# First projection chunk by halves, and the conv front end prepared in the last chunk of the projection

## What is computed

```python
x = layer_norm(x, ln0_g, ln0_b)
h = x @ w_in                                   # 1024 -> 384 value | 384 gate | 384 pool | 256 query
a = h_val * sigmoid(h_gate)
a = causal_depthwise_conv(a, conv_w, conv_b)   # 31 taps
a = silu(layer_norm(a, conv_ln_g, conv_ln_b))
p = pool_mixer(h_pool, pool_w, pool_scale)     # trailing means over 2, 4, 8, 16 frames
mo = memory_cross_attention(q, mem, w_mk, w_mv)  # 4 heads, 256 memory tokens
y = concatenate([a, p, mo]) @ w_out
x = layer_norm(alpha * x + y, ln1_g, ln1_b)
y = conv_ffn(x, w_up, ffn_conv_w, ffn_conv_b, w_down)
x = layer_norm(alpha * x + y, ln2_g, ln2_b)
```

## Time and profile before

| | |
|---|---|
| median of 3 runs | 2025.26 us (2025.09 to 2026.36) |
| profiled execution | 2024.7 us, its span 2023.0 us |
| mean granted TensorE clock | 0.978 |
| TensorE matmul busy | 1887.1 us, 93% of the span |
| VectorE / ScalarE / GpSimd busy | 1484.2 / 941.1 / 264.1 us |
| costliest line | L2072, three groups of 1848 matmuls, 723 to 726 us busy each |

### The profile page before, as it was taken

The page is one execution under the profiler, slowest core; times in us unless marked ns, Lnnn a source line. Parts: engine busy times, 40 slices in busy tenths (PEclk is TensorE's granted clock), DMA queues, the critical chain, the costliest instruction groups (busy, mean ns, idle before and its releaser), DMA issues.

```text
span 2023.0 us, 26054 instructions
## 1 busy us (share of the span) xinstructions
PE 1887.1 (93%) x8626; PEld 1563.7 (77%) x8626; DVE 1484.2 (73%) x1892; ACT 941.1 (47%) x1598; POOL 264.1 (13%) x339
## 2 busy tenths in 40 slices
PE   4999988869999899999999899999999897999997
PEld 4778868748878778888888688888887686887786
DVE  6444018658888798888887888787787767657899
ACT  3111114545555466556556655555556335234331
POOL 1111014101212322222221011000000000000111
PEclk9999999979999999999999899999999998999999
DMA  6432125444353743433434333122124567547543
GB/s 218 156 110 68 47 71 188 151 141 147 114 181 112 275 161 128 142 139 130 145 135 172 140 132 128 73 93 83 73 93 162 182 212 271 187 151 273 185 160 125
DMA packets 171786, 296.12 MB, mean 146 GB/s; under 512 B 11712, under 2 KB 106176, under 8 KB 171712
## 3 DMA queue, kind: packets, MB, share of 16 engines
q1 hardware_dynamic: 171712, 295.18, 41.9%
HBM read 189.23 MB, written 105.91 MB: 146 GB/s over the span
## 4 chain that ended last, share of the span: by engine, by line
PE 64%; DVE 12%; DMA 3%; issue 3%; ACT 3%; POOL 0%; SPq 0%; DVEq 0%; ACTq 0%; POOLq 0%
PE banks L2072 55%; PE banks L967 4%; DVE mov_lo L2269 1%; PE banks L985 1%; DMA mov_raw<-wdown_sums_scratch 1%; DVE sta_lo L2265 1%; PE banks L949 1%; PE banks L900 1%; DMA y_scratch<-up_and_out 1%; DMA mov_raw<-x_operands 1%; PE banks L931 1%; DVE up_and_out L2303 1%; DVE probs L1436 1%; PE banks L1030 0%; DVE up_and_out L2300 0%
## 5 line engine op out<-in xcount | busy, mean ns | idle before, releaser
L2072 PE MATMUL banks<-mov_hi,sta_hi 128*128 128x512 f32 x1848 | 726.3, 393 | 37.9 <-ACT banks L2148 19.6
L2072 PE MATMUL banks<-mov_lo,sta_hi 128*128 128x512 f32 x1848 | 723.5, 392 | 0.0
L2072 PE MATMUL banks<-mov_hi,sta_lo 128*128 128x512 f32 x1848 | 723.4, 391 | 0.0
L2072 PEld LDWEIGHTS banks<-mov_hi,sta_hi 128*128 128x128 f32 x1848 | 350.0, 189 | 117.3 <-ACT banks L2148 21.3
L2072 PEld LDWEIGHTS banks<-mov_hi,sta_lo 128*128 128x128 f32 x1848 | 349.6, 189 | 73.5
L2072 PEld LDWEIGHTS banks<-mov_lo,sta_hi 128*128 128x128 f32 x1848 | 350.2, 189 | 72.4
L2265 DVE TENSOR_TENSOR sta_lo<-sta_raw,sta_hi 128x512 fp32r<-128x512 f32 (+1 forms) x340 | 224.1, 675 | 61.2 <-ACT sta_hi L2134 59.3
L2134 ACT ACTIVATE sta_hi<-sta_raw 128x512 fp32r<-128x512 f32 (+1 forms) x340 | 198.8, 611 | 133.9 <-PE banks L2072 102.2
L261 PE MATMUL wb<-x0t_hi,win_hi 128*128 128x512 f32 x352 | 140.5, 399 | 2.9 <-DVE x0t_lo L353 2.9
L261 PE MATMUL wb<-x0t_hi,win_lo 128*128 128x512 f32 x352 | 138.3, 393 | 0.0
L261 PE MATMUL wb<-x0t_lo,win_hi 128*128 128x512 f32 x352 | 138.1, 392 | 0.0
(11 more groups left out here) (219 smaller groups left out, 2692.6 us busy)
## 6 DMA issues: line engine op xcount, KB each, us to landing
sta_raw<-in_w_up SPq DMA_DIRECT2D x88, 512.0 KB, 4.1
hidden_scratch<-up_and_out SPq DMA_DIRECT2D x44, 512.0 KB, 2.6
y_scratch<-up_and_out SPq DMA_DIRECT2D x16, 1024.0 KB, 7.5
sta_raw<-hidden_scratch SPq DMA_DIRECT2D x32, 512.0 KB, 4.5
up_and_out<-y_scratch SPq DMA_DIRECT2D x16, 1024.0 KB, 4.9
x_operands<-x_operands_out SPq DMA_DIRECT2D x56, 256.0 KB, 4.2
mov_raw<-x_operands SPq DMA_DIRECT2D x14, 1024.0 KB, 6.9
mov_raw<-in_w_down SPq DMA_DIRECT2D x44, 256.0 KB, 4.7
```

Of the source, the lines that this page charges most:

```text
L2072: last = pe.matmul(psum, w, x, start=(start and k == 0 and i == 0), stop=(stop and k == m - 1 and i == 2), skip_group_check=True)
```

## The change

In block 1:

- SyncE issues weight pieces 0 to 3 ahead of x tiles 2 and 3.
- TensorE does `turn` 0 to 3, then `project_half(0)` and `project_half(1)` in place of the first four tiles of chunk 0: half of the frames (256 columns) at a time, and within it weight piece by weight piece (two input slices, four output tiles: 24 matmuls each), with `turn` 4 to 7 behind pieces 1 and 2 of the first half. ScalarE's and VectorE's orders follow. `turn` of chunk 1 comes in twos behind tiles 7 to 10, and VectorE does all four layer norms of chunk 1 before its eight low parts.
- In the last chunk SyncE loads taps, conv bias and pairs 0 to 3, GpSimd makes the block mask, ScalarE and VectorE split taps and pairs 0 to 2, and VectorE makes bands 0 to 9. The buffers of the two blocks are placed by hand so that these go where the projection has finished.
- SyncE's wait for the query stores goes from the end of block 1 into block 2, behind nothing and ahead of the loads of pair 4 and the memory tokens.

In block 2:

- What is done already falls away at its start. The ten band buffers are reused for bands 10 to 15, then three of them for the rest; bands 10 to 23 are made in steps 1, 2, 3 and 6 to 10. The first `w_out` slice to be loaded is another one.

```diff
-        def first_turn(c):
-            return 1 if c else JT - 2 * TT
+        def turns_behind(c, n):
+            if c + 1 == NCH:
+                return ()
+            if c == 0:
+                return (2 * (n - JT + TT), 2 * (n - JT + TT) + 1) if n >= JT - TT else ()
+            return (n - 1,) if 1 <= n <= 2 * TT else ()
...
-            load_w(0)
+            for i in range(4):
+                load_w(i)
             load_x(2)
-            load_w(1)
             load_x(3)
-            for i in range(2, 7):
+            for i in range(4, 7):
                 load_w(i)
...
+                if c + 1 == NCH:
+                    for i, s in enumerate(x0_stored):
+                        sp.wait_ge(s, 16 * len(range(i, SEQ // P, RING)))
+                    sp.wait_ge(tp_ready, 2 * SEQ // P)
+                    opening.load_taps(sp)
                 for t in range(CT):
...
                     store_gated(c, t)
+                    if c + 1 == NCH and t == 0:
+                        sp.wait_ge(glu_stored[0], 16 * NCH)
+                        for m in range(4):
+                            opening.load_pair(sp, m)
...
-            sp.wait_ge(q_stored, 16 * QT * NCH)
...
+            def project_half(half):
+                tok = slice(half * CH // 2, (half + 1) * CH // 2)
+                pe.wait_ge(lo_done, TT * (half + 1))
+                for piece in range(4):
+                    pe.wait_ge(win_lo, piece + 1)
+                    for n in range(4):
+                        cols = slice(n * P, (n + 1) * P)
+                        for k in (2 * piece, 2 * piece + 1):
+                            pairs = exact_parts(w_hi[0][:, k, cols], w_lo[0][:, k, cols], xt_hi[0][:, k, tok], xt_lo[0][:, k, tok])
+                            for i, (w, x) in enumerate(pairs):
+                                last = pe.matmul(wb[:, n, tok], w, x, start=(k == 0 and i == 0), stop=(k == KT - 1 and i == 2), skip_group_check=True)
+                        if half and piece == 3:
+                            last.then_inc(proj, 1)
+                    if half == 0 and piece in (1, 2):
+                        turn(0, 2 * piece + 2)
+                        turn(0, 2 * piece + 3)
+
             pe.wait_ge(ident_ok, 2)
-            for i in range(2 * TT):
+            for i in range(TT):
                 turn(0, i)
+            project_half(0)
+            project_half(1)
             for c in range(NCH):
                 for n in range(JT):
-                    project(c, n)
+                    if c or n >= 4:
+                        project(c, n)
...
@@ ScalarE, block 1 @@
-            for u in range(TT):
-                weights_hi(u)
-                split_hi(0, 2 * u)
-                split_hi(0, 2 * u + 1)
-            for i in range(4, 7):
+            weights_hi(0)
+            weights_hi(1)
+            split_hi(0, 0)
+            split_hi(0, 1)
+            weights_hi(2)
+            split_hi(0, 2)
+            split_hi(0, 3)
+            for i in range(3, 7):
                 weights_hi(i)
+            for i in range(TT, 2 * TT):
+                split_hi(0, i)
...
@@ VectorE, block 1 @@
             layer_norm_end(0)
-            layer_norm(2)
             layer_norm_end(1)
             weights_lo(0)
             lows(0, 0, 1)
+            weights_lo(1)
+            lows(0, 2, 3)
+            layer_norm(2)
             layer_norm(3)
             layer_norm_end(2)
-            weights_lo(1)
-            lows(0, 2, 3)
+            weights_lo(2)
+            weights_lo(3)
             layer_norm_end(3)
-            weights_lo(2)
             lows(0, 4, 5)
-            weights_lo(3)
+            weights_lo(4)
             lows(0, 6, 7)
-            for i in range(4, 7):
+            for i in range(5, 7):
                 weights_lo(i)
...
+                if c + 1 == NCH:
+                    opening.taps_lo(dve, 0)
+                    opening.taps_lo(dve, 1)
+                    dve.wait_ge(opening.mask_made, 3)
+                    dve.wait_ge(proj, JT * c)
+                    for n in range(4):
+                        opening.conv_band(dve, n)
                     gate(c, 0)
+                    gate(c, 1)
+                    dve.wait_ge(proj, JT * c + 4)
+                    for n in range(4, 7):
+                        opening.conv_band(dve, n)
+                    opening.clear_leads(dve)
+                    gate(c, 2)
+                    for m in range(3):
+                        opening.pair_lo(dve, m)
+                    dve.wait_ge(proj, JT * c + 8)
+                    for n in range(7, 10):
+                        opening.conv_band(dve, n)
+                    continue
...
@@ VectorE, block 2 @@
+            bands_at = {1: (10, 11), 2: (12, 13), 3: (14, 15), 6: (16, 17), 7: (18,), 8: (19,), 9: (20, 21), 10: (22, 23)}
             for m in range(NP):
-                if is_conv(m):
-                    conv_band(2 * ORDER[m] + 3)
-                    conv_band(2 * ORDER[m] + 4)
+                for n in bands_at.get(m, ()):
+                    conv_band(dve, n)
```

More of the change, by code:

```diff
@@ L234, in _ @@
                 pool.tensor_tensor(s[:, 14:15], s[:, 13:14], half[:, 0:1], ALU.pow).then_inc(ln_rstd, 1)
+            pool.wait_ge(x0_stored[0], 16 * len(range(0, SEQ // P, RING)))
+            pool.wait_ge(tp_ready, 2 * SEQ // P)
+            opening.block_mask(pool)
         @block.tensor
@@ L323, in _ @@
                             weights_hi(i)
[L324 to L326 removed]
+                    for i in turns_behind(c, n):
+                        split_hi(c + 1, i)
+                    if c + 1 == NCH and n == 0:
+                        opening.taps_hi(act, 0)
+                        opening.taps_hi(act, 1)
+                    if c + 1 == NCH and n == 5:
+                        for m in range(3):
+                            opening.pair_hi(act, m)
         @block.vector
@@ L546, in mixing_phase @@
         last_xt = sem("last_x1T_stored")
-        ffn = ffn_phase(a, xop_d, x1_d, h_d, wdt_d, part_d, out, at, sem, banks)
-        block = ctx.enter_context(nc.Block())
         wo_more = late[:, 0:2 * D].rearrange("p (a d) -> p a d", a=2)
@@ L609, in groups_done, with band_place, band_before @@
             return 2 * ORDER.index(n // 2) + n % 2 + 1
+        def band_place(n):
+            return n if n < 10 else n - 10 if n < 13 else (3, 4, 5)[n - 13] if n < 16 else (n - 16) % 3
+        def band_before(n):
+            return max((g for g in range(n) if band_place(g) == band_place(n)), default=None)
         def bank_of(m):
@@ new lines, in block_mask @@
+        def block_mask(pool):
+            pool.memset(same, 1.0).then_inc(bands, 1)
+            pool.wait_ge(bands, 1)
+            same_cr = same.rearrange("p (c r) -> p c r", r=PHASES)
+            pool.affine_select(out=same_cr, in_=same_cr, compare_op=ALU.is_ge, fill=0.0, base=0,
+                               pattern=[[-PHASES, GROUP], [0, PHASES]], channel_multiplier=1).then_inc(bands, 1)
+            pool.wait_ge(bands, 2)
+            pool.affine_select(out=same_cr, in_=same_cr, compare_op=ALU.is_ge, fill=0.0, base=PHASES - 1,
+                               pattern=[[PHASES, GROUP], [0, PHASES]], channel_multiplier=-1).then_inc(bands, 1)
@@ new lines, in conv_band @@
+        def conv_band(dve, n):
+            dve.wait_ge(gt_lo, 1 + (n >= TAPS_FIRST))
+            if band_before(n) is not None:
+                dve.wait_ge(g_mm, groups_done(band_before(n)))
+            out = gt[band_place(n)][:, :].rearrange("p (e c r) -> p e c r", c=GROUP, r=PHASES)
+            tap = tap_parts[:, n, :, :].rearrange("p e (s o r) -> p (e s) o r", o=1, r=PHASES).to_broadcast((P, 2 * LAGS, GROUP, PHASES))
+            mask = same.rearrange("p (o c r) -> p o c r", o=1, r=PHASES).to_broadcast((P, 2 * LAGS, GROUP, PHASES))
+            dve.tensor_tensor(out, tap, mask, ALU.mult).then_inc(gt_ok, 1)
@@ L645, in _ @@
+        opening = Opening(load_taps, load_pair, block_mask, bands, taps_hi, pair_hi, taps_lo, clear_leads, pair_lo, conv_band)
+        q_stored = project_phase(nc, a, x0_d, cp_d, mix_d, used, at, banks, opening)
+        ffn = ffn_phase(a, xop_d, x1_d, h_d, wdt_d, part_d, out, at, sem, banks)
+        block = ctx.enter_context(nc.Block())
         @block.sync
```

208 lines of the change are left out of this document (90 added, 118 removed).

## The result

| | before | after |
|---|---|---|
| median of 4 runs on one chip | 2025.57 us (2025.09 to 2026.36) | 2012.50 us (2009.71 to 2015.45) |
| ratio, 95% interval | | 0.9935 [0.9920, 0.9950] |
| profiled execution, its span | 2024.7, 2023.0 us | 2015.45, 2013.7 us |
| mean granted TensorE clock | 0.978 | 0.976 |

The change makes the kernel 13.1 us faster; forecast were 13.7 us and 2011.5. The profiled execution is the slowest of the four of after. Its chain of waits is still TensorE's (`PE 64%`), so the up-projection sets most of the time as before.

What follows compares the result with a forecast made beforehand. TensorE bounds the kernel, mostly in an untouched up-projection, so gains come from its idle or slow stretches before about 345 us. Opening 6.3 plus boundary 7.4 is 13.7 us, giving 2011.5; likeliest range 2009 to 2014, 8 in 10 2006 to 2018.

Steps and rivals of the forecast that it cites:

- 6.3 + 7.4 = 13.7: Sum of the forecast gains: 6.3 us from the opening of block 1, 7.4 us from the boundary of the blocks.
- Ladder start, step by step: Opening: half-tile matmuls start at 21.0 in place of 33.4, chunk 1 at 98.2 in place of 104.5; worth 6.3 us.
- The last chunk's work is free: Last projection chunk: moved bands (15 us) and smaller work hide beside dense matmuls under some 25 us of cover; cost nothing.
- Block 2 starts 1.9 behind the projection's end, pair 0 0.9 later: Boundary: block 2 starts at 293.95 on the old clock, pair 0 at 294.9 in place of 301.45.
- I take no fall: Boundary: TensorE idles 2.8 us before pair 0 yet keeps its high clock; boundary worth 7.4 us.
- the prediction's other branch: Boundary: the clock also falls at 294.9, before pair 0, and the boundary is worth 5.3 us.
- Keys low: Keys: after 5 us idle the 48 matmuls run at the low clock for 4.7 us and lose 2.0.
- Values at the high level: Values: start at 335.4 for 342.81, 7.4 us earlier, and from there on the shift stays.
- Cold ladder: Rival, opening: all of half 0 and 5 us of half 1 at low pace; opening worth 0.6 us, 2017; chance 0.12.
- Slower reads from the moved buffers: Rival, projection: weights and x parts read slower from new places; 2031 if the pace rises by 0.02 us; chance 0.04.
- Only one place pays: Rival, boundary: keys stay put through late weights or a drain opening the block; 6.3 + 2 to 3, 2016.5; chance 0.13.

Runs made afterwards that it cites:

- the repeat: The changed kernel itself, unedited, run once more on the chip of the first group; 2012.70 us, ratio 0.9930 to the kernel before.
- no_early_prep: Changed kernel with taps, bands, mask and pairs prepared at the start of block 2 again, late query wait kept; 2020.41 us, ratio 0.9963 to before.
- old_opening: Changed kernel with the old order of loads, norms, splits and transposes and full tiles in chunk 0, the rest kept; 2019.51 us, ratio 0.9967 to before.
- piece6_last: Changed kernel with ScalarE copying weight piece 6 behind splits 4 to 7 in place of ahead; 2008.64 us, ratio 0.9909 to before.
- keys_before_bands: Changed kernel with VectorE making bands 10 to 15 behind the keys' low parts, in steps 3 and 4; 2007.04 us, ratio 0.9898 to before.
- order_only: Changed kernel with the edits of piece6_last and keys_before_bands together, no dummy transposes; 2003.79 us, ratio 0.9888 to before.
- fill_boundary: Changed kernel with 14 unused identity transposes behind the last projection matmul; 2008.31 us, ratio 0.9913 to before.
- query_wait_back: Changed kernel with the query stores waited for at the end of block 1 again, early preparation kept; 2017.54 us, ratio 0.9954 to before.
- fillers: Changed kernel with unused identity transposes in four waits: 20 in the opening, 14 at the boundary, 30 before keys, 12 before values; 2002.93 us, ratio 0.9883 to before.

## Why the prediction was right, and where not

Its mechanism and its sum held: 6.3 + 7.4 = 13.7 forecast; 6.7 at chunk 1 and 6.3 more by the values measured, and 13.1 between the medians. That the medians come so near is partly luck. By the first `w_out` matmul the trace of after has 12.1 us and the repeat 13.8, by the end 9.3 and 12.1; landing times and clock levels that the prediction did not know move each execution by 1 to 3 us. By its steps:

- *Ladder start, step by step.* Start 20.82 (21.0), second piece through at 29.2 (29.0), wait of 2.78 behind the late weight piece (2.3), fall of the clock there, four tiles ready at 53.0 (53.5), a wait of 1.11 for the third transposes (1.1), chunk 1 at 97.80 (98.2). Two errors in it cancel: the transfer of piece 6 took 4.1 us in place of 3.0, but the low pace set in only behind the transposes and ended at 40.3 in place of 41.8. Right, and shown by undoing it (6.8 us) and by taking the stall alone away (4.2 to 5.5).
- *The last chunk's work is free.* Right; that it must be there is shown by no_early_prep.
- *Block 2 starts 1.9 behind the projection's end, pair 0 0.9 later.* 2.1 and 0.85: right.
- **"I take no fall" at the boundary: the step that failed.** I had reasoned from the earlier trace rows, where the pace was high behind 3.01 us after dense work. Here the clock fell in both traces of the changed kernel, in old_opening and in piece6_last, and stayed up in keys_before_bands and order_only, each time behind 3.00 or 3.01 us. That row was one draw of something that goes either way: in old_opening the same place has 3.09 us, and the clock fell. The four transposes that I read could not have told, since a fall can come later: in after it came 1.2 us behind the restart. Only the matmuls behind them tell. The price: the four pairs took 16.05 us in place of 14.4, keys came 23.7 behind the end in place of 22.2, values 44.4 in place of 43.3. fill_boundary, without the fall, has its values at 43.3 too. So the fall cost 1.1 us by the values, where the prediction's other branch had 2.1 (5.3 us for the boundary; it is 6.3).
- *Keys low.* Wait 4.69 (5), 48 matmuls in 7.88 (5.8 + 2.0): right.
- *Values at the high level.* Not said outright, but the shift was to stay from there. Before, TensorE was idle 2.15 us there (the prediction's 2.6 is misread) and kept the clock; now it was idle 2.07 and did not, and 48 matmuls take 7.50 in place of 6.0. The shift falls from 13.0 at their start to 11.5 at their end and is 12.3 again at the next long wait (374.90 for 387.21), so this is most of the 0.9 us lost up to the first `w_out` matmul (13.0 to 12.1).
- *The rivals.* Cold ladder: no, the pace rose at 26.7. Slower reads from the moved buffers: no, chunk 1 to the end takes 187.6 us in both. Only one place pays: no, 6.8 us go with the ladder, 7.7 with the preparation (5.3 by its trace).

The experiments' expectations erred more than the prediction did. I had priced the two halves of the boundary by adding: 4 for the preparation and 2.5 for the late wait. They measured 7.7 and 4.8 when either was taken out. By the keys' distance from the projection's end, the preparation is worth 3.4 us without the late wait and 6.9 with it, and the late wait nothing without the preparation and 3.4 with it. The rest of the 4.8 is not found: by the first `w_out` matmul the trace has 2.0, and the remainder is within the intervals.

In "TensorE: Matmul & The Clock Gate", section on HAM oscillation, the Trainium skill tells of bursts of matmuls parted by waits for transfers, where each burst starts cold. The traces agree in part. Behind 4.69 us after was slow from the first matmul; behind 2.78, 3.00 and 2.07 us the burst started fast and the fall came up to 1.2 us later; and behind 3.0 us at the boundary four traces have a fall and two don't. As a rule for which wait costs something here it says too much, as a list of places to look at it was better than my reading of one row.

Open stays what decides between the two levels behind an idle stretch of 2 to 3 us. Length alone doesn't: 2.03 and 2.18 before the keys kept the clock, and so did 2.15 before the values in before and in no_early_prep; 2.07 before the values lost it in all eight traces that have it, so chance alone doesn't decide there either. The shortest up to there that lost it is 1.87 us, in the ladder of query_wait_back. Stretches filled to 1.5 us or less kept it each time: the boundary in the four kernels with transposes there, keys and values in fillers. Where the late waits for `y_scratch` come from was not tried either.

## What to carry to other kernels

When a stage is moved forward, look for the instruction that doesn't belong to the critical operand but stands in front of it in an engine's program: one line that put a late weight behind the splits was worth 4 us more on top of the 13. Two edits at one boundary can be worth little alone and much together, so price them as a chain of waits and not as a sum. And in a TensorE-bound kernel count each idle stretch of 2 to 3 us as its length plus a possible fall of the clock, some 1.5 to 2 us more for the dense work behind it, whatever one earlier row showed. To see whether it fell, read the starts well behind the restart and not the first few.

## What the hardware showed beside this

- The same idle stretch of 3.00 us at the same place gave a clock of 0.63 in one kernel and 1.00 in another in which TensorE does the same work there (windows above).
- Transposes of a resident identity hold the clock at 0.11 to 0.12 us apiece (76 in 8.46 us) and cost nothing when the engine would wait anyway; those at the boundary alone brought 4.1 us (2012.4 by the ratio of the repeat, 2008.3), although the four pairs gained only 1.5 and keys 1.6. The trace has 3.1 by the first `w_out` matmul, and the rest lies within the intervals.
- A load of 100 KB asked for beside two stores of 256 KB took 3.9 us to land; one of 80 KB, asked for after them, took 1.9. Piece 6 (256 KB) took 2.7 to 4.7 us in kernels that ask for it at the same point.
